# Root-mean-square norm: sums of squares with tokens on partitions, factors spread by TensorE

## What is computed

```python
def rms_norm(x, gain):
    xf = x.astype(jnp.float32)
    y = xf * lax.rsqrt(jnp.mean(xf * xf, axis=-1, keepdims=True) + EPS)
    return (y * gain.astype(jnp.float32)).astype(x.dtype)

def modulate(h, shift, scale):
    return h * (1.0 + scale) + shift
```

## Time and profile before

| what | value |
|---|---|
| median of 3 runs | 1553.81 us (1550.15 to 1558.1) |
| the profiled execution, its own time | 1553.5 us |
| its span, first to last instruction | 1551.7 us |
| mean granted TensorE clock | 0.990 of full speed |
| TensorE matmul / VectorE / ScalarE / GpSimd busy | 95% / 50% / 33% / 5% of the span |
| chain of work that ended last | TensorE 72%, DMA 20%, VectorE 5%, ScalarE 2% |

### The profile page before, as it was taken

One profiled execution on the slowest core, in us unless ns is written; L12 is line 12 of the kernel. 1 busy time (PEld: TensorE's weight loads), 2 busy tenths in 40 slices (PEclk: granted clock), 3 DMA queues, 4 the chain that ended last, 5 costly groups with the idle time before them and its releaser, 6 DMA issues.

```text
span 1551.7 us, 21231 instructions
## 1 busy us (share of the span) xinstructions
PE 1468.5 (95%) x8642; PEld 1061.6 (68%) x8642; DVE 769.3 (50%) x1418; ACT 507.7 (33%) x1019; POOL 79.1 (5%) x78
## 2 busy tenths in 40 slices
PE   5999999999999999989999999899999998889987
PEld 3566878878787798878899997798344443334433
DVE  0336766667654886665454677785222211212103
ACT  2324222222444444454444564463111111101102
POOL 0201000000200241001000000010000000000000
PEclk9999999999999999999999999999999999999999
DMA  8793554554323343113765456539899999999994
GB/s 340 277 357 134 210 190 160 215 190 163 139 98 127 139 185 142 56 34 126 278 243 190 150 179 244 189 109 380 368 425 426 427 426 427 425 428 425 427 426 192
DMA packets 54567, 390.50 MB, mean 252 GB/s; under 512 B 6064, under 2 KB 6208, under 8 KB 8000
## 3 DMA queue, kind: packets, MB, share of 16 engines
q1 hardware_dynamic: 53888, 387.72, 63.0%
q10 hardware_dynamic: 576, 1.36, 0.2%
HBM read 388.01 MB, written 1.05 MB: 251 GB/s over the span
## 4 chain that ended last, share of the span: by engine, by line
PE 72%; DMA 20%; DVE 5%; ACT 2%; issue 1%; SPq 0%; DVEq 0%; ACTq 0%
PE twin L813 47%; DMA ring<-in_wblk 19%; PE twin L1392 9%; PE twin L753 2%; PE twin L733 2%; PE twin L1279 1%; DVE wlo L2097 1%; PE twin L1090 1%; PE twin L1380 1%; PE twin L824 1%; PE twin L1026 1%; PE twin L1050 1%; DVE rst L2150 1%; PE twin L1444 1%; DMA xnat<-in_xnat 1%
## 5 line engine op out<-in xcount | busy, mean ns | idle before, releaser
L2097 DVE TENSOR_TENSOR wlo<-ring,whi 128x512 fp32r<-128x512 f32 (+1 forms) x396 | 260.1, 706 | 138.2 <-ACT whi L1547 135.4
L1547 ACT ACTIVATE whi<-ring 128x512 fp32r<-128x512 f32 (+1 forms) x408 | 225.1, 612 | 191.9 <-PE twin L813 124.9
L813 PE MATMUL twin<-Hh,whi 128*128 128x256 f32 (+1 forms) x848 | 280.6, 331 | 6.3 <-DVE wlo L2097 4.1
L813 PE MATMUL twin<-Hl,whi 128*128 128x256 f32 (+1 forms) x848 | 278.0, 328 | 0.0
L813 PE MATMUL twin<-Hh,wlo 128*128 128x256 f32 (+1 forms) x848 | 277.9, 328 | 0.0
L1392 PE MATMUL twin<-ring,xg 128*64 128x512 f32 x888 | 229.2, 596 | 25.6 <-DMA ring<-in_wblk 21.0
L813 PEld LDWEIGHTS twin<-Hh,whi 128*128 128x128 f32 x848 | 161.9, 191 | 31.2 <-issue 10.2
L1392 PEld LDWEIGHTS twin<-ring,xg 128*64 128x64 f32 x888 | 73.0, 137 | 153.0 <-issue 150.5
L813 PE MATMUL twin<-hsp,whi 128*128 128x512 f32 (+1 forms) x704 | 173.0, 338 | 0.9 <-DVE hsp L2244 0.9
L813 PEld LDWEIGHTS twin<-Hh,wlo 128*128 128x128 f32 x848 | 161.8, 191 | 14.0
L813 PEld LDWEIGHTS twin<-Hl,whi 128*128 128x128 f32 x848 | 161.9, 191 | 13.5
(11 more groups left out here) (363 smaller groups left out, 2091.4 us busy)
## 6 DMA issues: line engine op xcount, KB each, us to landing
ring<-in_wblk SPq DMA_DIRECT2D x336, 1024.0 KB, 9.4
small<-in_wblk SPq DMA_DIRECT2D x13, 1024.0 KB, 26.0
tmp<-in_wblk SPq DMA_DIRECT2D x13, 1024.0 KB, 26.1
xnat<-in_xnat SPq DMA_DIRECT2D x4, 512.0 KB, 7.1
xT<-in_xin SPq DMA_DIRECT2D x1, 2048.0 KB, 11.5
ring<-in_wblk SPq DMA_DIRECT2D x4, 512.0 KB, 3.7
out<-hTm SPq DMA_DIRECT2D x2, 512.0 KB, 3.0
small<-in_small SPq DMA_DIRECT2D x1, 738.0 KB, 7.6
```

Of the source, the lines that this page charges most:

```text
L813: t = e.matmul(out, a, b, start=start and n == 0, stop=stop and n == 2)
L1547: e.activation(hi, w, ACT.Copy).then_inc(*s_hi.up(m, h))
L2097: e.tensor_tensor(lo, w, hi.bitcast(F32), ALU.subtract).then_inc(*s_lov.up(m, h))
```

## The change

The sums of norms 1 to 4 are made by products in which the squares of 128 tokens are the stationary matrix and 8 columns of ones move, so that a token lies on a partition and each tile of 128 tokens has 8 equal columns. ScalarE takes the root of 128 x `n/128` values, VectorE the reciprocal. VectorE (even tiles) and ScalarE (odd tiles) scale an identity matrix of 128 x 128 by each tile's factors, and TensorE multiplies ones with it (`spread_factors`), which puts the factors on all partitions in PSUM bank 6. VectorE reads them there. `warm` becomes 1 + 2 in norm 1, 2 in norm 2, and 1 in norms 3 and 4. In both FFNs a square root of one column is put between the last two SiLUs and the first high parts. Norms 0, 5 and 6 stay as they are.

```diff
--- before.py
+++ after.py
@@ -325,6 +325,9 @@
         NORM_A[6, 0] = col("gfin", 0, 8)
         NORM_DST = (None, FH[0], AH, FH[1], XH, hM, hM)
         SUM_BANK = (None, 5, 3, 5, 3, 5, 4)
+        FACTOR_BANK = 6
+        nfac = tiny[:, 208:212]
+        FACTOR_DIAG = (None, part(FHID[0][:, 19, :], 0, 4, P), part(att, 8192, 4, P), part(att, 4096, 2, P), part(FHID[1][:, 10, :], 0, 4, P))
 
 
 
@@ -409,6 +412,11 @@
         s_sqv = signal("squares_dve", [(r, c) for r in range(1, 5) for c in range(1, KC, 2)] + [(5, c) for c in range(KC)])
         s_sum = signal("sums", [(r,) for r in range(1, 7)])
         s_root = signal("roots", [(r,) for r in range(1, 7)])
+        s_factor = signal("norm_factors", [(r,) for r in range(1, 5)])
+        tiles = [(r, t) for r in range(1, 5) for t in range(NORM_N[r] // P)]
+        s_fdv = signal("factor_diagonals_dve", [x for x in tiles if x[1] % 2 == 0])
+        s_fda = signal("factor_diagonals_act", [x for x in tiles if x[1] % 2])
+        s_wide = signal("factors_spread", [(r,) for r in range(1, 5)])
         triples = [(r, c, s) for r in (1, 2, 3, 4, 6) for c in range(KC) for s in range(len(NORM_STREAMS[r]))]
         s_ny = signal("normed", triples)
         s_nh = signal("normed_high", [t for t in triples if t[0] < 6])
@@ -730,7 +738,12 @@
                     e.wait_ge(*s_sqv.at(r, c))
                 else:
                     e.wait_ge(*s_sqa.at(r, c))
-                t = e.matmul(bank[SUM_BANK[r]][:, 0:n], ones, NORM_SQ[r][:, c, 0:n], start=c == 0, stop=c == KC - 1)
+                if r == 6:
+                    t = e.matmul(bank[SUM_BANK[r]][:, 0:n], ones, NORM_SQ[r][:, c, 0:n], start=c == 0, stop=c == KC - 1)
+                else:
+                    for q in range(n // P):
+                        t = e.matmul(bank[SUM_BANK[r]][:, 8 * q:8 * q + 8], NORM_SQ[r][:, c, q * P:(q + 1) * P], ones[:, 0:8], start=c == 0 and q == 0,
+                                     stop=c == KC - 1, skip_group_check=True)
             if cs[-1] == KC - 1:
                 t.then_inc(*s_sum.up(r))
 
@@ -772,6 +785,15 @@
 
             def sums(r, cs=range(KC)):
                 pe_sums(e, r, cs)
+
+            def spread_factors(r):
+                for q in range(NORM_N[r] // P):
+                    if q % 2:
+                        e.wait_ge(*s_fda.at(r, q))
+                    else:
+                        e.wait_ge(*s_fdv.at(r, q))
+                    t = e.matmul(bank[FACTOR_BANK][:, q * P:(q + 1) * P], ones, FACTOR_DIAG[r][:, q, :], start=True, stop=True)
+                t.then_inc(*s_wide.up(r))
 
 
             def router(cs):
@@ -880,7 +902,9 @@
                     sums(1, range(4))
             ada_cols(2)
             sums(1, range(4, KC))
-            warm(6, 7)
+            warm(1, 7)
+            spread_factors(1)
+            warm(2, 7)
 
             def ffn(layer, around, after_chunk, after_block):
                 n = FN[layer]
@@ -1095,7 +1119,8 @@
             ada_rows(6, range(2))
             sums(2, range(4, KC))
             ada_rows(6, range(2, 3))
-            warm(5, 6)
+            spread_factors(2)
+            warm(2, 5)
             first_units()
             UNIT_ROWS = {3: (3,), 5: (4,), 6: (5,), 8: (6,), 9: (7,)}
             for u in range(3, 12):
@@ -1146,7 +1171,8 @@
             def around(x):
                 ada_rows(7, range(2, 3) if x else range(2))
                 if x:
-                    warm(3, 6)
+                    spread_factors(3)
+                    warm(1, 4)
 
             def after_chunk(p, m):
                 if m and 2 <= p < 7:
@@ -1284,7 +1310,8 @@
             ada_rows(8, range(2))
             sums(4, range(4, KC))
             ada_rows(8, range(2, 4))
-            warm(2, 2)
+            spread_factors(4)
+            warm(1, 2)
 
             e.wait_ge(*s_xv.at("wll"))
             ws = parts(("win", 0), KC)
@@ -1564,6 +1591,14 @@
             def root(r):
                 n = NORM_N[r]
                 e.wait_ge(*s_sum.at(r))
+                if r < 5:
+                    q = n // P
+                    e.activation(nfac[:, 0:q], bank[SUM_BANK[r]][:, 0:8 * q].rearrange("p (t x) -> p x t", x=8)[:, 0, :], ACT.Sqrt, bias=eps,
+                                 scale=1.0 / D).then_inc(*s_root.up(r))
+                    e.wait_ge(*s_factor.at(r))
+                    for t in range(1, q, 2):
+                        e.activation(FACTOR_DIAG[r][:, t, :], ident, ACT.Copy, scale=nfac[:, t:t + 1]).then_inc(*s_fda.up(r, t))
+                    return
                 e.activation(rst[:, 0, 0:n], bank[SUM_BANK[r]][:, 0:n], ACT.Sqrt, bias=eps, scale=1.0 / D).then_inc(*s_root.up(r))
 
             def high(r):
@@ -1665,6 +1700,7 @@
                                     e.wait_ge(*s_hid.at(layer, 2 * bp - 2 + m))
                                 e.activation(sil[:, m, 0:n], bank[(4 * bp + m) % 6][:, 0:n], ACT.Silu).then_inc(*s_sil.up(layer, bp, m))
                         if (bp, what) == (10, 0):
+                            e.activation(tiny[:, 204:205], eps, ACT.Sqrt)
                             for k in range(nsp):
                                 high_pair(0, k)
                         after_fin(2 * bp + what)
@@ -2147,9 +2183,18 @@
             def normed(r):
                 n = NORM_N[r]
                 e.wait_ge(*s_root.at(r))
-                e.reciprocal(rst[:, 0, 0:n], rst[:, 0, 0:n]).then_inc(*own_v.up())
-                e.wait_ge(*own_v.now())
                 pair = 1 <= r < 5
+                if pair:
+                    q, wide = n // P, bank[FACTOR_BANK]
+                    e.reciprocal(nfac[:, 0:q], nfac[:, 0:q]).then_inc(*s_factor.up(r))
+                    e.wait_ge(*s_factor.at(r))
+                    for t in range(0, q, 2):
+                        e.tensor_scalar(FACTOR_DIAG[r][:, t, :], ident, nfac[:, t:t + 1], None, ALU.mult).then_inc(*s_fdv.up(r, t))
+                    e.wait_ge(*s_wide.at(r))
+                else:
+                    wide = rst[:, 0, :]
+                    e.reciprocal(rst[:, 0, 0:n], rst[:, 0, 0:n]).then_inc(*own_v.up())
+                    e.wait_ge(*own_v.now())
 
                 def low(c):
                     layer, chunk6 = NORM_MOD[r]
@@ -2162,7 +2207,7 @@
                 for c in range(KC):
                     for s, (a, b) in enumerate(NORM_STREAMS[r]):
                         y = (hM if r == 6 else NORM_SQ[r])[:, c, a:b]
-                        e.scalar_tensor_tensor(y, xT[:, c, a:b], NORM_A[r, s][:, c:c + 1], rst[:, 0, a:b], ALU.mult, ALU.mult).then_inc(*s_ny.up(r, c, s))
+                        e.scalar_tensor_tensor(y, xT[:, c, a:b], NORM_A[r, s][:, c:c + 1], wide[:, a:b], ALU.mult, ALU.mult).then_inc(*s_ny.up(r, c, s))
                     if pair and c:
                         low(c - 1)
                 if pair:
```

## The result

| | before | after |
|---|---|---|
| median of 20 runs each | 1553.64 us (1548.17 to 1559.36) | 1560.01 us (1556.95 to 1563.68) |
| ratio after to before, 95% interval | | 1.0041 [1.003, 1.0053] |
| the profiled execution: own time, span | 1553.5, 1551.7 | 1559.7, 1557.9 |
| mean granted TensorE clock | 0.990 | 0.984 |

A forecast was written before the change was run, and what follows sets the result against it. Bound: TensorE's dense products up to the experts, then DMA of expert weights from 1236 us. 1553.5 - 5.0 (norms) + 1.5 (early root) + 6.1 (clock) = 1556.1, said as 1556 us; range 1548 to 1561.

The forecast's parts named there:

- The class: Whole kernel: a change within about 0.5% (7.8 us), too small to tell from none, 85%; slower 13%, faster 2%.
- shorter root and reciprocal, all four norms, at full clock and without GpSimd: Root to first scaled chunk: 2.1 us gained in norm 1, 2.1 in norm 2, 0.8 in norm 3, nothing in norm 4.
- early root in layer 1: FFN of layer 1: table load and one-column root delay ScalarE's high parts, 1.5 us lost; covered in layer 0.
- low clock in and behind norm 1's first half: Norm 1, first half of the sums: one stay of 3.4 us at half speed, costing 1.5 us.
- low clock in norm 1's second half: Norm 1, second half: low clock stretches sums, filler and spreading, all on the path, costing 3.0 us.
- low clock in norm 2: Norm 2, both halves: two falls of 1.6 us, each in half of the executions, costing 1.6 us.
- the 11.3 us of clock cost: Whole kernel: the clock cost from which the long-stays rival would make the kernel measurably slower.
- passes with the factors in PSUM don't slow down: VectorE's passes in the norms: zero cost taken; bad end 0.05 us a pass, 0.9 us in all.
- The three places in the trace of before: Small-product stretches: heads' sums 1.8 us, clock 1.00; router 1065.76 to 1071.35, 0.83; 40 to 50 us, 0.66.
- The rival of the long stays: All four long sums: low clock held for twice 3.4 us, costing 13 us, time 1563.0 us; chance 12%.
- The rival "the clock holds": All four long sums: gate looks only at whether TensorE is busy, no clock loss, 1550.0 us; chance 25%.
- scaling of identities was put at 0.21 to 0.28 us each: Norms, behind the reciprocal: 0.21 us each, 0.28 for the first, from the heads' norm's 1.66 us for 8.

The follow-up runs named there:

- the combined kernel: Changed kernel with 128 columns of ones in the sums, no early root, and all diagonals made by ScalarE: 1549.87 us, ratio 0.9975 to before.
- the five narrow traces of the table: 8-column kernels: changed (1.0041), changed again (1.004), two-tensor diagonals (1.0039), changed without early root (1.0019), combined narrowed from 128 columns (1.0024).
- the three pairs of kernels that differ in nothing else: 128 against 8 columns in the sums: combined 0.9975 against 1.0024; without early root 0.9982 against 1.0019; with it 1.0032 against 1.0041.
- the second form tried here: Changed kernel with VectorE scaling the identities by scalar_tensor_tensor (two tensors) in place of tensor_scalar: 1559.63 us, ratio 1.0039.
- the wide kernel: Changed kernel with 128 columns of ones in the sums of norms 1 to 4 in place of 8, early root kept: 1557.56 us, ratio 1.0032.
- the other wide kernels: Changed kernel with 128 columns, no early root (0.9982); that with ScalarE making all diagonals (0.9975); that with norm 4's spreading between its modulation rows (0.9989).
- the one without the root: Changed kernel with 128 columns of ones in the sums and without the square root in the FFNs: 1551.43 us, ratio 0.9982.
- the last group: Third group of four versions timed on one chip; the kernel before had a median of 1553.81 us there.

## Why the prediction was right, and where it was not

The class was right (within 0.5%, 85%), and the 1560.0 lies in the range of 1548 to 1561, close to its end. The middle was 4 us low. That the result still lies inside is in part the width of the range: the costs came out at 2.5 us more for the clock and 2.3 for a wait that had been put at nothing, and 1.0 us less low clock in attention, which the change doesn't touch, offset a part. Step by step, for the profiled execution:

| term of the sum | forecast | measured |
|---|---|---|
| shorter root and reciprocal, all four norms, at full clock and without GpSimd | -5.0 | -4.8, see below |
| early root in layer 1 | +1.5 | +1.5 |
| low clock in and behind norm 1's first half | +1.5 | +3.3 |
| low clock in norm 1's second half | +3.0 | +2.4 |
| low clock in norm 2 | +1.6 | +2.9 |
| less low clock in attention | 0 | -1.0 |
| VectorE's diagonals wait for GpSimd | 0 | +2.3 |
| sum | +2.6 | +6.6, against 6.2 found |

How the right column is made: all but the early root are estimates from the rows above. The first row is not measured apart; it is the forecast less the 0.2 that norm 4 lost against before, and the combined kernel bears it out in size (root to scaled chunk shorter than before by 1.75, 1.74 and 0.53 us in norms 1 to 3, all the diagonals in a row on one engine). Norm 1's second half loses 1.2 in its sums (4.86 for 3.70) and 1.2 between root and chunk (3.61, less the 2.0 of the forecast, less 0.4 of waiting). Norm 2 loses 1.8 behind its first half and 1.1 in the spreading (2.07 for 0.98). The waiting is 0.89 - 0.48 in norm 1, 1.58 - 0.48 in norm 2 and 1.11 - 0.28 in norm 3. The 0.4 left over is not accounted for. (In the forecast, the 11.3 us of clock cost from which on a measurement would see the loss counts from 1553.5; against its own bound of 1561.6 it is 11.6.)

**What held.** The lengths of the new steps by the heads' norm; that the sums keep their length (3.74 and 1.85 us, at full clock); that passes with the factors in PSUM don't slow down (four in 1.66 us, against 1.67 in the earlier trace rows); norm 4; and the early root, covered in layer 0 and fully exposed in layer 1.

**What failed first: "In norm 2 I take two falls of 1.6, each in half of the executions", and one stay of 3.4 us for norm 1.** The three places in the trace of before were read as 1.8 us harmless and 5.6 harmful, with 3.7 between them. The runs show the low clock nearly always at 3.7 us of 8-column products: of the 20 long sums in the five narrow traces of the table 19 have it, 12 of them for 6.8 us. At norm 3, whose 1.9 us the forecast took as harmless, four of the five traces have one as well, though the other short sums have none. In the profiled execution the three terms measure 3.3, 2.4 and 2.9, together 8.6 us against 6.1 forecast. By the ratios the width is worth 7.6, 5.7 and 1.4 us in the three pairs of kernels that differ in nothing else. So the size was near, and the way to it was not: the low clock was taken to come in half the executions of norm 2, and to be short. The rival of the long stays (12%) had the lengths better, since three of the four last twice 3.4 us in this trace, but put their price at 13 us. Much of the agreement in size is therefore luck. The rival "the clock holds" (25%) is refuted, and with it a literal reading of the Trainium skill, page "TensorE: Matmul & The Clock Gate", section "What's actually happening", by which only how busy the engine is decides: in the windows above it is busy 10.00 of 10 us and loses the clock.

**What failed second: scaling of identities was put at 0.21 to 0.28 us each.** That price is from the heads' norm, at 1036 us, where GpSimd had ended its last piece at 1032.1 (in the earlier trace rows it is busy 1.04 of the 10 us). It was a price of VectorE alone, and it was used in stretches where VectorE is not alone. In norms 1 to 3 GpSimd works on one of its three blocks in just these stretches, in the kernel before as well. The Trainium skill, page "SBUF — State Buffer", section "Who interferes with whom", says that VectorE and GpSimd share a pair of ports, which one instruction holds to its end; it names `tensor_scalar` among the operations that can take the pair, and says that an instruction of VectorE with two inputs in SBUF, as the second form tried here has, contends with one of GpSimd that reads SBUF. This trace agrees: 0.28 us alone, 1.11 beside GpSimd. The ports themselves no run here shows. The reciprocal of the kernel before did not wait: it takes 1.75 us in norm 3, with GpSimd at work all the while, and 1.75 in norm 4 without it.

```profile
728.43 4.96 POOL L1992 TENSOR_TENSOR wlo<-ring,whi 128x512 fp32r<-128x512 f32 x4 [124.84 <-ACT whi L1547]
...
731.18 1.75 DVE L2150 RECIPROCAL rst<-rst 128x256 f32<-128x256 f32 x1 [2.87 <-ACT rst L1567]
...
939.50 1.75 DVE L2150 RECIPROCAL rst<-rst 128x256 f32<-128x256 f32 x1 [2.75 <-ACT rst L1567]
```

So the change put an instruction that waits in the place of one that does not.

**Open.** Pairs of kernels that differ by the early root alone differ by 3.3 us (before, with and without it), 3.4 (changed) and 7.8 (wide), by their ratios, while the traces show 1.5 at the place itself; layer 0 has none of it and layer 1 some 2.6. One ratio is uncertain by about 2 us to either side, so the first two may be 1.5 and chance; the third is not settled. It is the wide kernel with its six runs that stands out, since its gain over the changed kernel, 1.4 us by the ratios, is also far below the 5.7 and 7.6 that the same edit gave in the other two pairs. Its mean clock, 0.988, is below the 0.990 to 0.992 of the other wide kernels. Against the 0.992 of the one without the root that is some 10 us more at 1.2 GHz, an estimate of 3 to 4 us of time by the slopes in the last section. Where these executions lost the clock, the one trace kept does not show.

## What to carry to other kernels

In this kernel a product with 8 columns behind a full weight load took nearly as long as one with 128 (0.23 and 0.24 us), and a run of 16 such products lost TensorE's clock with 8 columns and kept it with 128 (one stay of 3.4 us was seen with 512, behind a wait): where the width costs so little, let 128 columns move. A small step that is to shorten a wait on VectorE is tried on ScalarE when GpSimd works beside it, and its price is to be read in the stretch where it will stand. An instruction that moves a table load "ahead of need" is judged by what waits for that engine at the new place: here 1.3 us were hidden before and exposed after.

## What the hardware showed that was not expected

- 32 records of sums take 3.74 us with 8 columns and 3.84 with 128; the first leave the clock at 1.2 GHz for 3.4 or 6.8 us, the second not once in four traces.
- Beside GpSimd's subtraction (four in 4.96 to 5.61 us), VectorE's scaling of 128x128 takes 0.70 to 1.39 us in the changed kernel instead of 0.28, and ends just behind one of GpSimd's instructions. ScalarE's copy with a scale keeps its 0.40 alone, 0.69 for two and 1.28 for four in a row.
- The executions of one kernel differ by some 10 us, and much of it goes with the clock: over the 33 runs of the kernel before in the last group, the time rises by 0.37 us for each us at the low clock (taken as twice the missing share of the mean clock times the time), over the 20 of the changed kernel by 0.31.
